# First scores of the dilated attention stage issued between the two tiles' values

## The reference, cut to what matters

```
for g, (window, dilation) in enumerate(DILATED_GROUPS):
    ...
    o, lse = dilated_group(proj[:, :, g, 0], proj[:, :, g, 1], proj[:, :, g, 2],
                           bias_g, dilation, radius)
...
    s = jnp.einsum('nbqhd,nbkhd->nbhqk', qb, kw).astype(jnp.float32) * (dh ** -0.5) + bias_blk
    smax = jnp.max(s, axis=-1, keepdims=True)
    p = jnp.exp(s - smax)
    denom = jnp.sum(p, axis=-1, keepdims=True)
    o = jnp.einsum('nbqhk,nbkhd->nbqhd', (p / denom).astype(v.dtype), vw)
...
wts = jax.nn.softmax(jnp.stack(lses, axis=0), axis=0)
o = jnp.einsum('gbsh,gbshd->bshd', wts.astype(h.dtype), jnp.stack(outs, axis=0))
```

## Time and profile before

| what | value |
| --- | --- |
| median of 3 runs | 3186.94 us (3185.25 to 3187.95) |
| profiled execution, its own time | 3185.09 us |
| its span | 3183.3 us |
| TensorE, share of the span busy | 91% |
| VectorE, share of the span busy | 54% |
| ScalarE, share of the span busy | 26% |
| mean granted TensorE clock | 0.979 of full speed |

### The profile page before, as it was taken

The page is one execution under the profiler, slowest core; times in us unless marked ns, Lnnn a source line. Parts: engine busy times, 40 slices in busy tenths (PEclk is TensorE's granted clock), DMA queues, the critical chain, the costliest instruction groups (busy, mean ns, idle before and its releaser), DMA issues.

```text
span 3183.3 us, 29811 instructions
## 1 busy us (share of the span) xinstructions
PE 2898.3 (91%) x10184; PEld 1631.6 (51%) x10184; DVE 1720.8 (54%) x3855; ACT 827.4 (26%) x2068; POOL 1213.8 (38%) x1117
## 2 busy tenths in 40 slices
PE   8689887898888988869879989999999999999998
PEld 4345333343333433323324767776676776544675
DVE  4586756867558675556653332222775762221664
ACT  3232212322123222212211321111342442121342
POOL 1487776877767767667761000000000002100000
PEclk9899999989999999989999999999999999999999
DMA  7899999999999999999995555663662752334551
GB/s 233 322 379 395 406 404 405 406 400 402 401 404 390 405 392 396 400 396 409 409 392 186 172 132 130 145 150 105 221 208 87 242 195 96 141 118 142 200 198 66
DMA packets 436209, 882.00 MB, mean 277 GB/s; under 512 B 54411, under 2 KB 219051, under 8 KB 435932
## 3 DMA queue, kind: packets, MB, share of 16 engines
q0 software_dynamic: 150112, 547.27, 43.7%
q1 hardware_dynamic: 282864, 332.52, 31.7%
q10 hardware_dynamic: 3084, 0.31, 0.1%
HBM read 878.85 MB, written 1.16 MB: 276 GB/s over the span
## 4 chain that ended last, share of the span: by engine, by line
PE 55%; DMA 15%; POOL 13%; DVE 7%; issue 5%; ACT 3%; SPq 1%; POOLq 0%; ACTq 0%; DVEq 0%
PE pb L1320 13%; PE pb L1222 8%; DMA arena<-in_peer_v,arena 8%; POOL arena L3507 6%; DMA arena<-in_peer_u,arena 6%; POOL arena L3520 6%; PE pb L580 6%; PE pb L1402 5%; PE pb L1527 5%; PE pb L720 4%; PE pb L1539 3%; PE pb L1372 2%; PE pb L599 2%; ACT arena L3235 2%; DVE arena L2289 2%
## 5 line engine op out<-in xcount | busy, mean ns | idle before, releaser
L1222 PE MATMUL pb<-arena,hT 128*128 128x512 f32 x2016 | 975.0, 618 | 182.6 <-DMA arena<-in_peer_v,arena 157.7
L1222 PEld LDWEIGHTS pb<-arena,hT 128*128 128x128 f32 x2016 | 369.9, 194 | 712.5 <-issue 630.3
L2289 DVE CUSTOM_DVE_ANT_0 arena<-arena,xn 128x1024 f32<-128x1024 f32 x410 | 502.5, 1233 | 336.8 <-DMA arena<-in_peer_u,arena 336.3
L3507 POOL DMA_INDIRECT arena<-in_peer_u,arena x512 | 567.4, 1108 | 201.2 <-issue 144.7
L3520 POOL DMA_INDIRECT arena<-in_peer_v,arena x512 | 555.4, 1085 | 216.4 <-issue 125.9
L3430 POOL TENSOR_TENSOR st<-st,mhalf 128x1 f32<-128x1 f32 (+1 forms) x46 | 34.9, 758 | 1470.3 <-DVE st L1796 1193.8
L720 PE MATMUL pb<-arena,hT 128*128 128x512 f32 x752 | 345.3, 601 | 14.8 <-DVE cells L1716 7.4
L1320 PE MATMUL pb<-arena 128*128 128x256 f32 x1280 | 287.0, 381 | 4.4 <-ACT arena L3201 3.2
L1320 PEld LDWEIGHTS pb<-arena 128*128 128x128 f32 x1280 | 243.3, 191 | 43.2 <-issue 9.9
L720 PEld LDWEIGHTS pb<-arena,hT 128*128 128x128 f32 x752 | 141.1, 193 | 185.5 <-issue 162.5
L1320 PE MATMUL pb<-arena,hT 128*128 128x256 f32 x960 | 220.4, 379 | 9.8 <-DMA arena<-in_ffn_w_up 7.7
(11 more groups left out here) (382 smaller groups left out, 2911.6 us busy)
## 6 DMA issues: line engine op xcount, KB each, us to landing
arena<-in_w_in SPq DMA_DIRECT2D x48, 1024.0 KB, 11.7
arena<-in_ffn_w_gate SPq DMA_DIRECT2D x44, 1024.0 KB, 5.3
arena<-in_ffn_w_up SPq DMA_DIRECT2D x44, 1024.0 KB, 7.9
arena<-in_ffn_w_down SPq DMA_DIRECT2D x44, 1024.0 KB, 9.8
arena<-in_attn_w_in SPq DMA_DIRECT2D x72, 512.0 KB, 6.7
arena<-in_peer_w_q SPq DMA_DIRECT2D x32, 1024.0 KB, 11.7
arena<-in_ret_w_in SPq DMA_DIRECT2D x16, 2048.0 KB, 7.8
arena<-in_w_out SPq DMA_DIRECT2D x16, 1024.0 KB, 11.7
```

The source lines that it names most:

```text
L1222: ins = nc.tensor.matmul(pb[:, 2 * t + half, :], diag[:, n % DIAGS, :], vrow[:, n % RING, half * CH:(half + 1) * CH], start=n % PICKS == 0 ...
L2289: V.tensor_tensor_reduce(out=row, in0=row, in1=xn[:, n // PICKS % NT, :] if n < first else pflat[:, 0:D], scale=1.0, scalar=0.0, op0=ALU.m ...
L3507: G.indirect_dma_start(out=urow[:, n % RING, :], out_offset=None, in_=table_u, in_offset=bass.IndirectOffsetOnAxis(ap=eid[:, u % 4, k:k + ...
```

## The change

On TensorE, `scores(0)` stands between `values(0)` and `values(1)` of pair 0, where before it followed both. On VectorE, `couple(0)` stands ahead of the copy of the second values. ScalarE's and SyncE's lists are the same. No instruction is added or removed.

```diff
@@ TensorE, dilated() @@
                 turned = []
-                for step in range(4):
+                for step in range(3):
                     projections(step)
                 scores(0)
+                projections(3)
                 for v in range(COUPLES):
@@ VectorE, dilated() @@
-                for step in range(4):
+                for step in range(3):
                     projections(0, step)
                 couple(0)
+                projections(0, 3)
                 for v in range(COUPLES):
```

## The result

The changed kernel takes 3179.33 us (median of 20 runs, 3171.49 to 3187.88) against 3187.28 us (20 runs, 3181.64 to 3191.70) for the kernel before. The ratio is 0.9975 with an interval of 0.9970 to 0.9981: 8.0 us less, between 6.1 and 9.6. The forecast of 3180.9 us had the right direction, and the measured time lies within its range. Its gain of 6.08 us is about a quarter smaller than this 8.0. The case called likeliest, "within 0.2%" (6.4 us), did not come by the median, though the near end of the interval, 6.1 us, still lies inside it.

The account below looks back on a forecast made before the run. TensorE, busy 91% of the span, was taken to bound the kernel. Waits of 4.39 us plus 1.69 us for the clock gave 6.08 us, so 3186.94 - 6.08 = 3180.9 us, range 3178.6 to 3183.8 us.

Parts of the forecast that it names:

- within 0.2%: Whole kernel: measured time within 0.2% (6.4 us) of the kernel before, chance 0.65.
- The wait: TensorE ahead of pair 0's first transposes: idle 4.08 us and 0.31 us for the softmax both go, gaining 4.39 us.
- The cover: Second values on TensorE hide the first softmax: first row ready with 1.08 us to spare, second with 0.11 plus 0.51 us.
- The rival of a slower couple beside the values: VectorE's couple 0 runs slower beside the second values, gain 2 to 4 us, 3183 to 3185 us; chance 0.10.
- The clock: TensorE behind the wait: the fall to half clock, 3.42 us in the profile, goes with the wait.
- Another 1.69 us: Eight transposes and next scores behind the wait take 2.10 us at full clock and not 3.79.
- the fall is usually longer: Rival: clock fall behind the wait usually lasts 10.24 us, so the gain is 9.5 us, 3177.4 us; chance 0.10.
- the lower case: Rival: gain is the wait alone, no clock fall in most executions of before, 4.39 us, 3182.6 us; chance 0.24.
- What comes after: Behind pair 1's first projection: all later work, with weight waits of 7.7 us in 4 waits, moves up as one piece.
- The slower rival: Slot 1's refill for pair 1 lands late; slower than before once it takes 20.1 us against 14.0; chance 0.03.

Follow-up runs that it names:

- the filled wait: Kernel before, with six unused matmuls of 384 columns added on TensorE behind the first scores; ratio 0.9997 to the kernel before.
- VectorE's half alone: Kernel before, with only couple 0 moved ahead of VectorE's copy of the second values, TensorE's scores still behind both tiles' values; ratio 1.0001.
- the head filled: Changed kernel, with six unused matmuls of 512 columns added in TensorE's wait at the head of the dilated stage; ratios 0.9968 and 0.9963 to the kernel before.
- TensorE's half alone: Kernel before, with only the first scores moved between the two tiles' values, VectorE still copying the second values ahead of couple 0; ratio 1.0002.

## Why the prediction was right, and where it was small

**The wait.** Predicted: 4.39 us go. Measured: no wait in any of four profiles. Both halves alone leave it (4.52 and 4.13 us), so the copy's move behind the couple was not only free, as predicted, but needed.

**The cover.** Predicted: the second head's row is ready 5.05 us behind the scores, 0.11 us ahead of the end of the second values, and has 0.51 us more. Measured: it is ready at 1932.22 (1931.73 + 0.49) and the second values end at 1932.53, so 0.31 us. The second values took 5.36 us and not 5.16, the scores 1.08 and not 1.13, and the eight transposes 0.87 and not 1.02. From the end of the first values to pair 1's first projection that adds up to the predicted 8.39 us exactly, which is luck: two misses of 0.15 us cancel. The rival of a slower couple beside the values has nothing for it: its operations take 0.43, 0.69 and 0.49 us, against 0.42, 0.69 and 0.49 alone. The first exponential started 1.12 us behind the table load, 1.1 forecast, and waited for VectorE.

**The clock.** The mechanism was right, by the filled wait: without the idle stretch there is no fall. **The size was off.** "Another 1.69 us" was taken from the one execution profiled, which had the shortest fall of the three with the old order. The filled wait shows what the old order takes at the full clock: 5.16 us of second values, 7.92 to pair 1's first projection and 20.92 for its projections (the changed kernel's row), 34.00 on the ruler. The three profiles of before read 35.41, 37.01 and 36.46, so the fall cost 1.4, 3.0 and 2.5 us, on average 2.3, and 2.4 in the kernel with VectorE's half alone. The other 0.3 us of the 1.69 are no clock at all: in the old order the eight transposes run in two pieces of 0.66 us, and the sum had priced them as one of 1.02. Waits and broken transposes are thus worth 34.00 - 29.30 = 4.7 us and the clock 2.3, and the gain at the place is 36.29 - 29.30 = 7.0 us.

All runs together say the same: the changed kernel has a mean of 3180.4 us in 49 runs, the kernel before 3187.6 in 127, a difference of 7.1 us with a standard error of 0.6. (The four sets of the changed kernel have means from 3179.1 to 3183.2 us, and two sets of before on one chip differ by 2.3, so the difference is less certain than that.) So the runs fit a worth of 7 us, nothing has to be looked for outside this stretch, and the first 20 runs' interval, 6.1 to 9.6, holds it. That 6.08 met 6.11 in the first pair of profiles says little of the size, since the sum was made from that same profile of before. The forecast rival "the fall is usually longer" had the right direction, but a fall of 10.2 us was the wrong row: 6.8 us was the longest seen at this place.

The rule of the Trainium skill that I weighed against the row ("TensorE: Matmul & The Clock Gate", section "What's actually happening": the same kernel shows different amounts of slow work from run to run) is borne out by these traces: 3.4, 6.8 and 6.8 us of half clock behind the same wait of 4.13 us. But I drew only the lower case from it, no fall and 4.39 us, and that case came in none of the five profiles with the wait, counting those with half of the change. The rule allows longer falls as well as none, and in three of the five the fall was longer than in the row.

**What comes after.** Predicted: the rest moves up as one piece. In the four profiles of the changed kernel the waits for the SwiGLU weights are 7.6 to 8.2 us in 4 waits, as in the earlier trace rows or half a microsecond more. The first of them:

```profile
PE pb L1320 <- DMA arena<-in_ffn_w_up: 7.6, 4, 2.2
```

**The slower rival.** Its place was real, its price was not. The refill of slot 1 has 14.0 us, and in the kernels with added matmuls it took from pair 1's first projection 14.5 us (1950.60 - 1936.07) with the first wait filled, and 14.8 us with the head filled, 14.3 in its second profile. So if the transfers take about as long in the changed kernel, its margin is close to none; it paid nothing for it in four profiles. Why the kernels with added matmuls did is open.

**The term that was mis-sized.** It is the sum's last, the 1.69 us for the work behind the wait: in its place the traces show 0.3 us for the broken transposes and 1.4, 3.0 or 2.5 us for the clock. With it went the call of "within 0.2%", which hung on the 0.3 us between 6.08 and 6.4.

## What to carry to other kernels

When an engine that works its list in order waits for a short chain on the others, look for independent work in its own list that can stand between the request and the use, and move the hand-over on the other engine too: either half alone was worth nothing here. A wait on TensorE cost more than its length here, since the clock fell behind it; take its price from several profiles, because one shows only one of several lengths. Once the cover was as long as the chain, more of it brought nothing, and the request ran into its own inputs.

## What the runs showed of the hardware

A wait of TensorE of 4.13 us (4.52 with TensorE's half alone) was followed by a half clock in all five profiles that had it, and none of the eight profiles without it had a half clock at this place. The fall began 3.5 to 4.8 us after TensorE ran dry in the three of the kernel before (1932.56 - 1929.06 in the third, 1937.44 - 1932.67 in the first), in two of them when it was at work again; it lasted 3.4 us once and 6.8 us twice, and cost 1.4 to 3.0 us. Unused matmuls of 4.14 us in the wait kept the clock at 1.00, and those of 5.32 us at the stage's head removed a fall of 10.2 us. The six blocks of pair 1's queries and keys, whose first part ran at half clock, took 22.5 and 22.0 us, at full clock 20.9.
